# A hybrid decoder step in f32: unit queue, border loads and block order of the MLP

## The reference

```python
h = hp + W_out [DilatedSWA || mLSTM](rms_norm(hp, norm1_g))
def sqrelu_mlp(h, w_up, w_down):
    u = jnp.einsum('btd,df->btf', h, w_up)                       # 1024 -> 4096
    return jnp.einsum('btf,fd->btd', jnp.square(jax.nn.relu(u)), w_down)
hp = hp + sqrelu_mlp(rms_norm(hp, norm2_g), w_up, w_down)
y  = rms_norm(hp, norm_f_g)
# outputs also: the key and value windows of prompt and samples (2048 rows of
# each of 8 sequences, shifted by 8), conv, C, n and m states
```

## Time and profile before

| | us |
|---|---|
| runs of the kernel before | 2995.04, 2988.67, 2995.75 (median 2995.04) |
| profiled execution | 2992.78, span 2991.0 |
| TensorE busy | 2737.8 |
| VectorE / ScalarE / GpSimd busy | 1834.0 / 1079.5 / 651.7 |

### The profile page before, as it was taken

The page is one execution under the profiler, slowest core; times in us unless marked ns, Lnnn a source line. Parts: engine busy times, 40 slices in busy tenths (PEclk is TensorE's granted clock), DMA queues, the critical chain, the costliest instruction groups (busy, mean ns, idle before and its releaser), DMA issues. The chain is left out here.

```text
span 2991.0 us, 46001 instructions
## 1 busy us (share of the span) xinstructions
PE 2737.8 (92%) x17331; PEld 2293.8 (77%) x17331; DVE 1834.0 (61%) x3890; ACT 1079.5 (36%) x1984; POOL 651.7 (22%) x539
## 2 busy tenths in 40 slices
PE   7999999999999978999879998888887999899996
PEld 5878788778777766678767886888776888778885
DVE  5522555233788755577566666555554777877776
ACT  4301322111676752423354554544443111321113
POOL 1212012120455440211100001000001344533333
PEclk9999999999999988999989998999999999999998
DMA  4464243444464548957567779576779677776762
GB/s 155 150 233 154 95 139 130 158 131 147 129 203 134 171 157 319 407 205 262 205 229 261 271 267 336 202 251 236 241 246 337 231 248 248 258 271 224 238 234 76
DMA packets 348899, 642.33 MB, mean 215 GB/s; under 512 B 39375, under 2 KB 237139, under 8 KB 328326
## 3 DMA queue, kind: packets, MB, share of 16 engines
q1 hardware_dynamic: 281516, 543.44, 52.6%
q10 hardware_dynamic: 66026, 91.95, 8.5%
q0 software_dynamic: 1152, 4.19, 0.4%
HBM read 461.65 MB, written 244.95 MB: 236 GB/s over the span
## 5 line engine op out<-in xcount | busy, mean ns | idle before, releaser
L2639 PE MATMUL bank<-mlp_h_hi,mlp_wu_hi 128*128 128x272 f32 (+1 forms) x1344 | 448.5, 334 | 83.5 <-ACT mlp_made L3013 47.8
L2640 PE MATMUL bank<-mlp_h_lo,mlp_wu_hi 128*128 128x272 f32 (+1 forms) x1344 | 443.6, 330 | 0.0
L2641 PE MATMUL bank<-mlp_h_hi,mlp_wu_lo 128*128 128x272 f32 (+1 forms) x1344 | 443.2, 330 | 0.0
L3293 DVE TENSOR_TENSOR mlp_acc<-mlp_acc,bank 128x512 f32<-128x512 f32 x440 | 300.2, 684 | 147.3 <-PE bank L2641 140.7
L2639 PE MATMUL bank<-mlp_wd_hi,mlp_u_hi 128*128 128x512 f32 x896 | 353.7, 395 | 36.0 <-DVE mlp_acc L3293 30.3
L2640 PE MATMUL bank<-mlp_wd_lo,mlp_u_hi 128*128 128x512 f32 x896 | 352.9, 394 | 0.0
L2641 PE MATMUL bank<-mlp_wd_hi,mlp_u_lo 128*128 128x512 f32 x896 | 352.6, 393 | 0.0
L2639 PEld LDWEIGHTS bank<-mlp_h_hi,mlp_wu_hi 128*128 128x128 f32 x1344 | 261.6, 195 | 114.5 <-issue 56.7
L3072 ACT ACTIVATE mlp_u_hi<-mlp_u_raw 128x768 fp32r<-128x768 f32 x126 | 113.0, 944 | 471.7 <-POOL mlp_u_raw L2936 471.3
L2640 PEld LDWEIGHTS bank<-mlp_h_lo,mlp_wu_hi 128*128 128x128 f32 x1344 | 261.9, 195 | 20.1
L2641 PEld LDWEIGHTS bank<-mlp_h_hi,mlp_wu_lo 128*128 128x128 f32 x1344 | 261.1, 194 | 20.0
(11 more groups left out here) (391 smaller groups left out, 5468.5 us busy)
## 6 DMA issues: line engine op xcount, KB each, us to landing
mlp_wd_lo<-wd SPq DMA_DIRECT2D x46, 1024.0 KB, 7.6
mlp_wd_hi<-wd SPq DMA_DIRECT2D x45, 1024.0 KB, 5.5
mlp_u_raw<-u SPq DMA_DIRECT2D x256, 128.0 KB, 2.3
out_win_k_sample<-in_cache_k SPq DMA_DIRECT2D x48, 680.0 KB, 7.2
out_win_v_sample<-in_cache_v SPq DMA_DIRECT2D x48, 680.0 KB, 6.4
mlp_wu_raw<-in_w_up SPq DMA_DIRECT2D x30, 1024.0 KB, 7.3
wd<-mlp_un_hi SPq DMA_DIRECT2D x32, 896.0 KB, 4.4
wd<-mlp_un_lo SPq DMA_DIRECT2D x32, 896.0 KB, 7.3
```

The lines of the kernel that those rows point to most:

```text
L2639: nc.tensor.matmul(out, ah, bh, start=fresh and k == 0, stop=False, skip_group_check=not fresh)
L2640: nc.tensor.matmul(out, ah, bl, start=False, stop=False, skip_group_check=not fresh)
L2641: ins = nc.tensor.matmul(out, al, bh, start=False, stop=k == n - 1, skip_group_check=not fresh)
L3293: v.tensor_tensor(a, a, b[:], ALU.add).then_inc(summed, 1)
```

## The change

- **Raw loads of units** are issued by ScalarE (`load_unit` in its block), behind the same wait for the stores; in a set of the first group between the first and second part of the split of the next up weights.
- **Units** follow phases of half a set: load at one phase, sums, high part and the high part's store at the next, low part and its store at the one after. Sets 0 to 14 have one unit each as before; from set 18 on a unit comes every three phases.
- **Cache copies**: 45 in the up stage as before, but two in each of sets 1 to 6, none in sets 13 to 17 and from 44 on; three move out of one burst of nine and out of the output stage into the projection.
- **Kept weights**: only piece 1 is kept; piece 0 is loaded raw again.
- **Border loads**: the h loads at set 15 are split into halves, first the columns of q = 0. The four h loads at the end of the output stage go out one a tile (t = 11 to 14) instead of all at t = 11, and their sums one tile later.
- **First down weights** are loaded raw (2.1 MB) at set 46, summed on VectorE there, and split in set 47 (`first_down_hi`, `first_down_low`).
- **Steps**: blocks 6 and 7 of a group are interleaved, the samples' step stands last in a block, and their final norm last of all.

```diff
                 for c in range(2, 8):
                     sp.wait_ge(lo_ready, c + base)
                     sp.dma_start(wq_raw, K.w_qk[c]).then_inc(wq_in, 16)
-                    K.copy_cache(sp)
+                    for e in range(g + 1):
+                        K.copy_cache(sp)
...
-                            copies(GN[0] * (b - 2) + 3, 8 if b < 4 else 4)
+                            copies(GN[0] * (b - 2) + 3, 8)
...
-                        copies(40 + 3, 9)
...
-                if t == 11:
+                if 11 <= t < 15:
                     for q in range(2):
                         sp.wait_ge(M.h_out[q], 16 * 4)
-                    for q in (1, 3, 0, 2):
-                        M.load_h(sp, K, (0, 2, 4, 5)[q], q, 0, M.h_in[q])
+                    q = (1, 3, 0, 2)[t - 11]
+                    M.load_h(sp, K, (0, 2, 4, 5)[q], q, 0, M.h_in[q])
...
-                if 12 <= t < 16:
-                    h_sum(t - 12)
+                if 13 <= t < 17:
+                    h_sum(t - 13)
...
-    KEPT = (NC, NC + 1)
+    KEPT = (NC + 1,)
...
-    unit_sets = sorted(list(range(15)) + list(range(18, 45, 2)) + [27, 33, 39])
-    unit_at = {s: w for w, s in enumerate(unit_sets)}
+    EARLY = 15
+    phase = [2 * s for s in range(EARLY)] + [2 * 18 + 3 * w for w in range(UNITS - EARLY)]
+    unit_load = {at: w for w, at in enumerate(phase)}
+    unit_sum = {at + 1: w for w, at in enumerate(phase)}
+    unit_rest = {at + 2: w for w, at in enumerate(phase)}
...
+    ORDER = [(kb, p) for kb in range(6) for p in range(5)]
+    ORDER += [(6, 0), (6, 1), (6, 2), (7, 0), (6, 3), (6, 4), (7, 1), (7, 2), (7, 3), (7, 4)]
...
-            if s - 1 in unit_at:
-                store_unit(unit_at[s - 1])
-            if s in unit_at:
-                load_unit(unit_at[s])
+            for ph in (2 * s, 2 * s + 1):
+                if ph in unit_rest:
+                    store_unit(unit_rest[ph], 1)
+                if ph in unit_sum:
+                    store_unit(unit_sum[ph], 0)
+            if s < 13 or 18 <= s < 44:
+                for e in range(2 if 1 <= s < 7 else 1):
+                    K.copy_cache(sp)
             if s == LAST - 1:
                 sp.wait_ge(mm, 7 * s)
+                for j in range(2):
+                    for e in range(2):
+                        sp.dma_start(wd_raw0[:, 0:7:2, j, 256 * e:256 * e + 256], K.ins["w_down"][0, j, e].rearrange("p (a c) -> p a c", a=4))\
+                            .then_inc(wd_first, 16)
...
+        def load_unit(w):
+            kb, j, e = unit_of(w)
+            if w:
+                act.wait_ge(un_out, 32 * w)
+            act.dma_start(un_raw[:, 0:7:2], K.ins["w_down"][kb, j, e].rearrange("p (a c) -> p a c", a=4)).then_inc(un_in, 16)
...
+        def first_down_hi(k):
+            sl = slice(2 * k, min(2 * k + 2, 7))
+            act.wait_ge(wd_t, 2)
+            act.wait_ge(mm, 7 * LAST + k + 1)
+            A(wd_hi[0][:, sl], wd_raw0[:, sl], ACT.Copy).then_inc(wd_hi_ready, 1)
...
             if early:
                 w_hi(ci + 1, 0)
+            if 2 * s in unit_load:
+                load_unit(unit_load[2 * s])
+            if early:
                 w_hi(ci + 1, 1)
...
             if s == 15:
                 sp.wait_ge(mm, 7 * s + 1)
-                M.load_h(sp, K, 0, 0, 1, M.h_in[0])
+                M.load_h(sp, K, 0, 0, 1, M.h_in[0], 0)
...
+                M.load_h(sp, K, 0, 0, 1, M.h_late[0], 1)
+                M.load_h(sp, K, 1, 1, 1, M.h_late[1], 1)
+                M.load_h(sp, K, 2, 3, 1, M.h_late[4], 1)
```

More of the change, by code:

```diff
@@ L1745, in __init__ @@
         self.h_in = [sem(f"mlp_h_in{q}") for q in (0, 2, 4, 5)]
+        self.h_late = [sem(f"mlp_h_late{q}") for q in range(5)]
         self.h_mid, self.h_s = sem("mlp_h_mid"), sem("mlp_h_s")
@@ L2711, in mlp @@
     own, pool_own = M.own, sem("mlp_pool_own")
-    wd_first = [sem(f"mlp_wd_first{q}") for q in range(4)]
+    wd_first, wd_t, wd_hi_ready, wd_lo_ready = (sem("mlp_wd_" + n) for n in ("first", "t", "hi", "lo"))
     wd_in = [[sem(f"mlp_wd_in{b}{q}") for q in range(4)] for b in range(2)]
@@ L2736, in mlp @@
-    N = len(steps)
-    ends = steps[-1].mm0 + 7
-    pair = {st.m: st for st in steps if st.p is not None}
-    first_of = {st.kbi: st for st in reversed(steps)}
-    samp = {st.kbi: st for st in steps if st.p is None}
-    M_END = 64
-    def nth(F):
-        return 4 if F is None else F + (F >= 4)
+        for kb, p in ORDER:
+            if g == 0 and p == 4:
+                continue
+            st = Step()
+            st.g, st.kb, st.p, st.kbi, st.n = g, kb, p if p < 4 else None, 8 * g + kb, len(steps)
+            st.m = sum(a.p is not None for a in steps) if p < 4 else None
+            st.before = max((a.n for a in steps if a.g == g and a.p == st.p), default=None)
+            st.mm0 = steps[-1].mm0 + (3 if steps[-1].p is None else 7) if steps else 7 * S0
+            st.po0 = steps[-1].po0 + (3 if steps[-1].p is None else 7) if steps else 0
+            st.F = 4 * g + p if kb == 7 and p < 4 else None
+            steps.append(st)
@@ new lines, in mlp @@
+    pair = {st.m: st for st in steps if st.p is not None}
+    samp = {st.kb: st for st in steps if st.p is None}
+    final = {st.F: st for st in steps if st.F is not None}
+    M_END = len(pair)
+    SAMPLES = 8
+    down_at, samples_at, convert_at = {}, {}, {}
+    for kbi in range(1, 16):
+        users = [st.n for st in steps if st.kbi == kbi]
+        free = max((st.n for st in steps if st.kbi == kbi - 2), default=-1) + 1
+        for q in range(4):
+            down_at.setdefault(free + q * (users[0] - free) // 4, []).append((kbi, q))
@@ L2746, in nth_raw @@
+    for kb in range(8):
+        at = samp[kb - 1].n + 1 if kb else final[2].n
+        samples_at[at], convert_at[at + 1] = kb, kb
     def nth_raw(ci):
-        return ci if ci < NC else ci - len(KEPT)
+        return ci - sum(k < ci for k in KEPT)
     def mm_end(st):
@@ L2774, in piece @@
         return q * n, n
-    kept_out, kept_in = sem("mlp_kept_out"), [sem(f"mlp_kept_in{e}") for e in range(2)]
+    kept_out, kept_in = sem("mlp_kept_out"), sem("mlp_kept_in")
     block = K.ctx_mlp.enter_context(nc.Block(no_gpsimd_drain=True))
@@ L2950, in _ @@
             before = steps[st.n - 1] if st.n else None
-            if before and before.kb == 7 and before.p is not None:
-                gains(4 * before.g + before.p)
+            if before and before.F is not None and before.F < 7:
+                gains(before.F)
     @block.scalar
@@ L3054, in _ @@
                 hi_of(1, 1, 0)
-            if s == LAST:
+            squares(s, 2)
+            if g == 0 and 2 * s + 1 in unit_sum:
+                unit_hi(unit_sum[2 * s + 1])
+            squares(s, 3)
+            if s == LAST - 1:
                 act.wait_ge(u_sums, 4)
@@ L3233, in _ @@
             up_post(s, 1)
+            if g == 1 and s > 16:
+                unit_work(2 * s)
             if s in (16, 17):
@@ L3284, in down_post @@
                 if i == 0:
-                    dve.wait_ge(summed, steps[st.n - (4 if st.g == 0 else 5)].po0 + 7)
+                    dve.wait_ge(summed, steps[st.before].po0 + 7)
             elif i == 2:
@@ L3308, in final_sums @@
         def final_sums(F):
-            st = pair[28 + F if F < 4 else 60 + F - 4]
-            dve.wait_ge(summed, st.po0 + 7)
+            dve.wait_ge(summed, final[F].po0 + 7)
             a = acc[:, F % 4]
```

269 lines of the change are left out of this document (128 added, 141 removed).

## The result

The changed kernel takes **3068.7 us** (median of 4 runs, 3059.3 to 3072.2) against 2993.1 us (4 runs): **1.0249 times the time of the kernel before, 95% interval 1.0221 to 1.0277**. I had forecast 3014, range 2955 to 3055. The direction was right, the size was not: 76 us lost where I had 19, and the time lies outside the range.

The account below looks back on a forecast made before the run. TensorE, busy 92%, was taken to bound the kernel, in first-group sets with 0.9 us to spare over the unit loop. Terms summed to +19 us on 2992.8, 3011.8, or 3014 with the median 2.3 higher; range 2955 to 3055.

Parts of the forecast that it names:

- Units in the first group, +42: Up stage, first group: sets take the lengthened unit loop's time, 24.0 us with two copies, 21.9 with one; +42 us.
- Units in the second group, -2: Up stage, second group: about 20 us a unit, 388 against 390 us; -2 us, ends -53 and +40.
- 2 to 3 us for what they miss: Second group: allowance per unit for high and low parts having fixed places, among others behind up-weight splits.
- 17 x 20 + 4.5 sets x 10.6: Second group's time: 17 units at 20 us plus 4.5 sets of matmuls at 10.6 us, giving 388 us.
- units at 22.5: Rival: second-group units at 22.5 us, first-group loop 23 to 25, granted clock falling; +40 more, 3055; chance 0.15.
- low store alone: Second group: the 4.4 us for a low store in the unit's 15.9 us with every engine free.
- Where rows and notes met: Second group: raw load on ScalarE's queue passes SP's backlog, landing in 4.3 to 5 us; otherwise near 7.6, costing +40.
- Start of the up stage +3: Up stage start: about 1 MB more ahead of set 1's up weights and kept weights; +3 us (-3 to +8).
- border -1: Border between the groups: earlier halves and fewer loads against added VectorE work and a later last unit; -1 us (-10 to +6).
- Out stage -7: Out stage: h loads spread over four tiles remove most of a 14.6 us VectorE wait; -7 us (-12 to 0).
- Projection -4: Projection: removing a burst of nine copies ahead of a weight load saves TensorE time; -4 us (-7 to 0).
- Down stage, 0 - 8 - 4: Down stage: 0 for first down weights made on chip, -8 us for interleaved blocks 6 and 7, -4 at the end.

Follow-up runs that it names:

- f1: Changed kernel with, in the first group, the low store first on SP's queue, and raw loads issued by SP again: 3023.7 us, 1.0105.
- a2: Changed kernel with the raw loads of w_down back on SP's queue, each right behind the low store of the unit before: 3046.8 us, 1.0188.
- a3: Changed kernel with the second group's units at the sets of the kernel before, each loaded at its set's start: 3029.1 us, 1.0129.
- a4: Changed kernel with the low part of the second group's units at an earlier place on VectorE: 3037.0 us, 1.0155.
- c1: Changed kernel with all units as in the kernel before, except that the high store waits for the high part alone: 2922.1 us, 0.9774.
- b1: Kernel before with one edit, a unit's high store waiting for the high part alone: 2950.7 us, 0.9869.
- b2: Kernel before with only the projection's copies spread out of their burst and the out stage's h loads one a tile: 2968.6 us, 0.9937.
- d1: c1 with the down stage's blocks in plain order, 6 and 7 not interleaved, samples still last: 2918.5 us, 0.9755.
- c2: Changed kernel, first group's units as before; second group's still 1.5 sets apart, low part early, SP raw loads behind low stores, copies behind those: 2944.4 us, 0.9855.

## Why the prediction was right or wrong

- **Units in the first group, +42: right in the loop, short by 12, wrong in how it reaches TensorE.** The sets stood 24.8 us apart with two copies (24.0 forecast), 22.7 with one (21.9), and there were seven of the latter where I counted six. The low store landed 14.9 us after the high part with two copies (14.5 forecast) and 12.9 with one (12.4). But I had VectorE wait near 10 us a set for raw loads: it was 1.8, and 6.6 for the up weights, which SP's queue held behind the high store; TensorE was busy 89% there, not 85%. f1 adds what I had not seen: behind this loop stood a second one, by the up weights.
- **Units in the second group, -2: the step that failed.** The loop was 23.1 us, not 20. By its pieces: the low part's place 5.6 us where I took 2.0 plus part of "2 to 3 us for what they miss"; low store 6.9 against 6.3; raw load 6.0 against 4.3; landing to high part 4.5 against 5.2. I had bounded the places by a feeling and not by the rows, though the order of VectorE's instructions was there to be read: it put the low part behind three parts of a split. The sum "17 x 20 + 4.5 sets x 10.6" was of the right form, with 16 loops and 62 us around them (11.3 ahead, 50.7 behind) in place of 17 and 48. Taken back alone, the raw load's queue gives back 22 us of the stretch (a2), the plan 37 (a3), the low part's place 28 (a4); with all units as before it takes 345.0 us (c1). Of my rivals, "units at 22.5" (chance 0.15) came nearest, though not by waits of over 5 us in each set: TensorE's waits for ScalarE and VectorE there were 25 in 29 sets, the longest 5.9. Its 3055 is 14 us short, 12 in the first group and about as much in the second, less what the other stages won.
- **What I never priced alone was the best part of it.** I took TensorE's pace and the loop as near level in the second group and never added up the loop before there: 21.5 us. b1 shows that it paced sets 18 to 44 before as well: 2.3 us less a loop took 39 us off the stretch. The early high store stood in my sum only as "low store alone"; by itself it takes 40 us off the kernel. The earlier trace rows said so: 47.8 us of TensorE's waits hung on that chain.
- **Where rows and notes met.** I took 4.3 to 5 us for a raw load on a queue of its own. Of the changed kernel's 17 in the second group, the 8 with no up weights on their way landed in 4.4 us on the mean, the 9 issued 1 to 5 us behind up weights on SP's queue in 7.4; on the same queue, in the kernel before, it was 4.5 in 6 and 7.7 in 11. One of the 9, in 8.1 us:

```profile
1955.43 0.61 SPq L2801 DMA_DIRECT2D mlp_wu_raw<-in_w_up  x1
...
1957.09 0.55 ACTq L3027 DMA_DIRECT2D mlp_un_raw<-in_w_down  x1
...
1965.24 0.43 DVE L3210 TENSOR_TENSOR mlp_un_raw<-mlp_un_raw 128x256 f32<-128x256 f32 x1 [2.94 <-DMA mlp_un_raw<-in_w_down]
```

  The Trainium skill, "Trainium Kernel Development and Optimization", section "Key Constraints", says that several issuers save only the issue time; these 17 loads bear it out, and I had bet on the other. In a2, with the raw load back on SP's queue, it landed no later: 5.4 us on the mean, 6.0 in the changed kernel.
- **Start of the up stage +3, border -1:** +4.7 and -1.4, right.
- **Out stage -7:** -11.1, within its -12 to 0. **Projection -4:** -13.8, and -12.0 alone in b2, outside its -7 to 0: I counted the idle time and not the clock behind it.
- **Down stage, 0 - 8 - 4:** -12.3 in sum, where I had -12: luck. It was for other reasons, and three kernels with the old down stage show 703.0 to 708.2 us, nine with the changed one 695.3 to 699.9, so about -9. Blocks 6 and 7 gave nothing (d1): idle time around them was 13.0 us and is 11.8. At the start TensorE's wait fell from 14.5 to 10.1 us, gain_f still its cause, as said (POOL waits 26.3 us for it). At the end the time behind the last product fell from 21.2 to 13.6 us, while waits ahead of it grew from 5.5 to 11.3. These pieces make 6 us; where the rest comes from, and what the first down weights made on chip are worth alone, was not tried.

The waits of the changed kernel at the start of the down stage, answering to the earlier trace rows, and in the out stage where the earlier trace rows had 14.6 us:

```profile
POOL mlp_u_raw L2939 <- DMA mlp_gain_f<-in_norm_f_g: 26.3, 1, 26.3
...
PE bank L2641 <- DVE mlp_acc L3345: 10.1, 1, 10.1
```

```profile
DVE out_st L1693 <- DMA out_mb<-mix: 2.6, 2, 1.9
```

A kernel that beats both stands at 2909.4 us, 0.9725 of the time before: the loads of the change, its weights made on chip and its samples at the end, the units as before with the early high store, plain blocks, gain_f's wait late. Two buffers for a unit might take the loop apart; the memory around the one is taken up by live tiles, and it was not tried.

## What to carry to other kernels

Cut a serial loop at its events (store issued, landed, load issued, landed, computed) and add the pieces before judging who paces a stage; in the second group it paced sets 18 to 44 while TensorE looked 86% busy. On a queue served in order, let each store go when its own data is ready, and keep it together with what the loop waits for: copies and other loads belong behind the load, not between two stores. A plan in finer steps did not help here even with its places mended (c2): it ended two sets earlier and left 21 us more behind its last unit.

## What the runs showed of the hardware

- Two stores of 0.92 MB issued 0.6 us apart: the second lands after 7.3 us on the mean; with the first 2.6 us ahead on the mean (b1), after 5.3. The first one's head start of 2.0 us more comes back whole.
- A 0.5 MB load on a second queue does not pass a 1 MB load that is 1 to 5 us ahead on the first: 7.4 us on the mean of 9, against 4.4 of 8 without it.
- Idle time of 7.1 us in the projection cost 12 us: the granted clock was 0.96 for the 52 us around it (1.00 in b2), and the same matmuls took 4.9 us more of busy time.
